# Weight halves for a layer chain: a tile for every weight sum, low parts of down pieces by adding transfers, six whole tiles first

## The reference

```python
def sq_relu_mlp(h, w_up, w_down):
    return jnp.square(jax.nn.relu(h @ w_up)) @ w_down          # hidden width 4096
...
x = x + sq_relu_mlp(rmsnorm(x, mlp_norm[layer]), w_up[layer], w_down[layer])
```

```python
def conv_gated_mlp(n, w_up, conv_w, w_down):
    gate, up = jnp.split(n @ w_up, 2, axis=-1)                 # hidden width 2816
    gate = causal_dwconv(gate, conv_w)                         # 3 taps
    return (jax.nn.silu(gate) * up) @ w_down
```

## Time and profile before

| | |
|---|---|
| median of 3 runs | 2898.85 us (2897.19 to 2899.41) |
| profiled execution, its time | 2896.0 us |
| its span | 2894.2 us |
| PE busy | 2737.9 us (95%) |
| POOL busy | 1879.7 us (65%) |
| DVE busy | 2023.6 us (70%) |
| ACT busy | 1219.6 us (42%) |
| chain that ended last | PE 68%, DVE 22%, issue 5% |
| read from HBM | 249.52 MB |

### The profile page before, as it was taken

The page is one execution under the profiler, slowest core; times in us unless marked ns, Lnnn a source line. Parts: engine busy times, 40 slices in busy tenths (PEclk is TensorE's granted clock), DMA queues, the critical chain, the costliest instruction groups (busy, mean ns, idle before and its releaser), DMA issues.

```text
span 2894.2 us, 48195 instructions
## 1 busy us (share of the span) xinstructions
PE 2737.9 (95%) x18508; PEld 2470.3 (85%) x18508; DVE 2023.6 (70%) x3175; ACT 1219.6 (42%) x2145; POOL 1879.7 (65%) x2144
## 2 busy tenths in 40 slices
PE   9988999999899999999999889999999899988998
PEld 6767989877798988988899888999988799978887
DVE  8958666686666668897544777776797645767775
ACT  4454434455343444433343334445343353334442
POOL 6425998856599885532236589997542225489997
PEclk9999999999999999999999999999999999999999
DMA  5112332332233233323324122233322324122222
GB/s 185 59 34 75 96 110 94 111 102 75 72 100 105 95 117 111 110 66 96 105 83 133 54 81 93 91 100 108 100 78 88 89 87 142 60 86 84 88 90 93
DMA packets 122676, 271.25 MB, mean 94 GB/s; under 512 B 22864, under 2 KB 57040, under 8 KB 122192
## 3 DMA queue, kind: packets, MB, share of 16 engines
q1 hardware_dynamic: 73104, 245.98, 26.4%
q10 hardware_dynamic: 49344, 22.19, 2.8%
HBM read 249.52 MB, written 18.61 MB: 93 GB/s over the span
## 4 chain that ended last, share of the span: by engine, by line
PE 68%; DVE 22%; issue 5%; ACT 2%; POOL 1%; DMA 1%; ACTq 0%; SPq 0%; DVEq 0%
PE aux L1035 16%; PE acc L800 15%; PE acc L1090 13%; PE acc L1287 5%; PE acc L1094 3%; PE acc L849 3%; PE aux L1301 3%; DVE index_score L3227 2%; PE acc L1268 2%; PE aux L1268 2%; DVE best L3220 2%; DVE w_raw L2703 1%; DVE unit_b L3130 1%; POOL w_lo L772 1%; PE acc L833 1%
## 5 line engine op out<-in xcount | busy, mean ns | idle before, releaser
L772 POOL TENSOR_TENSOR w_lo<-w_raw,w_hi 128x256 fp32r<-128x256 f32 x1744 | 1478.5, 881 | 931.9 <-ACT w_hi L1535 928.1
L1535 ACT ACTIVATE w_hi<-w_raw 128x512 fp32r<-128x512 f32 (+2 forms) x680 | 487.2, 738 | 381.6 <-PE acc L800 143.7
L772 POOL TENSOR_TENSOR w_lo<-weight_sum,w_hi 128x256 fp32r<-128x256 f32 x396 | 407.2, 1054 | 61.2 <-ACT w_hi L1535 56.7
L1035 PE MATMUL aux<-token_sum_hi,w_hi 128*128 128x264 f32 (+1 forms) x1056 | 304.7, 289 | 77.6 <-ACT kept_product L1821 40.8
L800 PE MATMUL acc<-n_hi,w_hi 128*128 128x264 f32 (+1 forms) x1336 | 337.6, 317 | 8.8 <-DVE unit_a L3136 6.5
L800 PE MATMUL acc<-n_lo,w_hi 128*128 128x264 f32 (+1 forms) x1336 | 326.6, 309 | 0.0
L800 PE MATMUL acc<-n_hi,w_lo 128*128 128x264 f32 (+1 forms) x1336 | 326.0, 308 | 0.0
L1035 PE MATMUL aux<-token_sum_hi,w_lo 128*128 128x264 f32 (+1 forms) x1056 | 300.5, 285 | 0.0
L1035 PE MATMUL aux<-token_sum_lo,w_hi 128*128 128x264 f32 (+1 forms) x1056 | 300.3, 284 | 0.0
L1035 PEld LDWEIGHTS aux<-token_sum_hi,w_hi 128*128 128x128 f32 x1056 | 201.0, 190 | 90.8 <-issue 67.0
L1090 PE MATMUL acc<-hidden_hi,w_hi 128*128 128x512 f32 x688 | 271.9, 395 | 2.1 <-DVE hidden_lo L3109 2.1
(11 more groups left out here) (525 smaller groups left out, 6364.3 us busy)
## 6 DMA issues: line engine op xcount, KB each, us to landing
w_raw<-in_stream SPq DMA_DIRECT2D x420, 512.0 KB, 3.6
unit_blocks<-unit_scratch ACTq DMA_DIRECT2D x26, 256.0 KB, 3.9
w_raw<-in_stream SPq DMA_DIRECT2D x16, 384.0 KB, 3.2
unit_scratch<-unit_staged ACTq DMA_DIRECT2D x20, 256.0 KB, 2.6
saved_x<-x SPq DMA_DIRECT2D x2, 2112.0 KB, 9.6
x<-saved_x SPq DMA_DIRECT2D x16, 264.0 KB, 2.7
saved_gates<-root ACTq DMA_DIRECT2D x12, 264.0 KB, 2.0
unit_scratch<-unit_staged ACTq DMA_DIRECT2D x1, 2560.0 KB, 15.1
```

Source lines behind the costliest of these rows:

```text
L772: i = pool.tensor_tensor(wl[:, slot, at + a:at + z], source[:, a:z], wh[:, slot, at + a:at + z].bitcast(F32), ALU.subtract)
L1035: mm = pe.matmul(aux[:, bank, 0:width], w[:, slot, at_ + P * b:at_ + P * b + P], v[:, b, :], start=(opens and b == 0 and i == 0), stop=(b ...
L1535: act.activation(wh[:, slot, at_:at_ + n], weights_of(o), ACT.Copy).then_inc(w_hi, 1)
```

## The change

It has four parts.

1. s3 gets a tile of its own (in `square_sum`, which these stages don't use), and a21 is no longer overwritten. In the FFN s3 of the next pair is made behind the second down half, in front of a22's work on DVE; in the MLP it stays at a22. A raw slot of a pair is loaded anew when the four sums are made and the low parts of its direct factors are.
2. The low part of a down half is not subtracted on POOL. ACT writes −w_hi (a rounded copy with scale −1) into `w_lo`, then w_hi; POOL issues a transfer that adds the raw weights from DRAM to it (`accum_op`), with four semaphores in turn, and TensorE waits for its landing. The raw slot is free once ACT has copied both parts.
3. `w_lo` counts only the entries that POOL still subtracts (`order.low`).
4. The MLPs begin with six whole tiles instead of four, and so have 13 pairs instead of 14; the first pair is followed by all eight down halves of the first chunk. DVE's order at the start is written anew. The banks of the down products are counted from the end of the stage.

Some semaphores are merged, two names into one, to make room; each waiter waits for the same event as before.

```diff
+MLP_WHOLE = 6
+def whole_tiles(stage):
+    return MLP_WHOLE if stage.startswith("mlp") else FFN_CHUNKS[0][1]
...
-    order = [("whole", 0, n) for n in range((2 if gated else 1) * chunks[0][1])]
+    order = [("whole", 0, n) for n in range((2 if gated else 1) * whole_tiles(stage))]
     for e in range(1, len(chunks)):
-        n = (chunks[e][1] - chunks[e][0]) // (1 if gated else 2)
+        a = max(chunks[e][0], whole_tiles(stage))
+        n = (chunks[e][1] - a) // (1 if gated else 2)
         for i in range(n):
-            order.append(("pair", e, i))
+            order.append(("pair", a, i))
             order += [("down", e - 1, k) for k in range(4 * i // n, 4 * (i + 1) // n)]
...
+    def parts_of(self, p):
+        return [n for n, (kind, piece, _) in enumerate(self.ops)
+                if (piece == p and kind in ("whole", "down", "a11", "a12")) or (piece == p - 1 and kind == "a22")]
...
+    sum_tiles = {"s1": weight_sum[:, 0, :], "s2": weight_sum[:, 1, :], "s4": weight_sum[:, 2, :], "s3": ssq[:, 0:KT // 2 * P]}
...
         for p in range(RAW_SLOTS, pieces):
-            sp.wait_ge(w_lo, order.freed(p - RAW_SLOTS))
+            q = p - RAW_SLOTS
+            last = order.parts_of(q)[-1]
+            if order.ops[last][0] == "down":
+                sp.wait_ge(w_hi, last + 1)
+            else:
+                sp.wait_ge(w_lo, order.low[last])
+            if q in order.sums or q - 1 in order.sums:
+                sp.wait_ge(w_sum, order.sums[q if q in order.sums else q - 1])
             load_piece(p)
...
+            if kind == "down":
+                d = order.sent[o] - 1
+                if d >= LOWS:
+                    pool.wait_ge(*low_landed(d - LOWS))
+                pool.wait_ge(w_hi, o + 1)
+                pool.dma_start(wl[:, slot, at:at + n], stream[p, :, part * n:part * n + n], accum_op=ALU.add)\
+                    .then_inc(low_landed(d)[0], 16)
+                continue
...
-                pe.wait_ge(w_lo, o + 1)
+                if kind == "down":
+                    pe.wait_ge(*low_landed(order.sent[o] - 1))
+                else:
+                    pe.wait_ge(w_lo, order.low[o])
...
+            if kind == "down":
+                act.activation(wl[:, slot, at_:at_ + n], weights_of(o), ACT.Copy, scale=-1.0)
             act.activation(wh[:, slot, at_:at_ + n], weights_of(o), ACT.Copy).then_inc(w_hi, 1)
...
-                i = dve.tensor_tensor(a21, a21, a11, ALU.subtract)
+                i = dve.tensor_tensor(s3, a21, a11, ALU.subtract)
...
             token_sum_low(stage, 0)
+            whole(2)
+            token_sum_low(stage, 1)
             weight_sum_of(stage, 0, "s1")
-            token_sum_low(stage, 1)
             weight_sum_of(stage, 0, "s2")
-            whole(2)
+            whole(3)
             token_sum_low(stage, 2)
             weight_sum_of(stage, 0, "s4")
             token_sum_low(stage, 3)
+            whole(4)
             weight_sum_of(stage, 0, "s3")
-            whole(3)
+            whole(5)
             low()
...
-                    weight_sum_of(stage, u + 1, "s3")
                     if u == feed["pairs"] - 1:
                         low()
                 elif kind == "down":
                     down(o, d, stage, last_rows(l))
                     d, since = d + 1, since + 1
-                    if since == 1:
-                        weight_sum_of(stage, pair + 1, "s4")
+                    if since in (1, 2):
+                        weight_sum_of(stage, pair + 1, ("s4", "s3")[since - 1])
```

More of the change, by code:

```diff
@@ L136 @@
 LATER = 2
+LOWS = 4
 STAGES = ["mix0", "mlp0", "mix1", "mlp1", "layer0", "layer1"]
@@ L172, in mlp @@
                 for i in range(2):
-                    column("w_up", layer, P * (MLP_CHUNKS[e][0] + 2 * n + i))
+                    column("w_up", layer, P * (e + 2 * n + i))
             else:
@@ L207, in block2 @@
                 for c in (0, FF2):
-                    column("w_up_2", layer, c + P * (FFN_CHUNKS[e][0] + n))
+                    column("w_up_2", layer, c + P * (e + n))
             else:
@@ L282, in __init__ @@
         self.index = {op: n for n, op in enumerate(self.ops)}
+        self.low, self.sent, low, sent = [], [], 0, 0
+        for kind, _, _ in self.ops:
+            low, sent = low + (kind != "down"), sent + (kind == "down")
+            self.low.append(low)
+            self.sent.append(sent)
+        self.sums, sums = {}, 0
+        for feed in self.feeds.values():
+            for q in feed["pieces"]:
+                sums += len(SUMS)
+                self.sums[q] = sums
     def used(self, n):
@@ L297, in half @@
         return self.place[o] // 2, KT // 2 * P * (self.place[o] % 2)
-    def freed(self, p):
-        found = [n + 1 for n, (kind, piece, _) in enumerate(self.ops) if piece == p or (piece == p - 1 and kind == "a22")]
-        paired = [n + 1 for n, (kind, piece, _) in enumerate(self.ops) if piece == p and kind == "s3"]
-        return paired[0] if paired else max(found)
+    def parts_of(self, p):
+        return [n for n, (kind, piece, _) in enumerate(self.ops)
+                if (piece == p and kind in ("whole", "down", "a11", "a12")) or (piece == p - 1 and kind == "a22")]
 PAD = 4
@@ L394, in build @@
     order = Order(plan, starts)
-    used, evicted, slot_of = order.used, order.evicted, order.slot
+    used, evicted, slot_of, lows = order.used, order.evicted, order.slot, order.low
     base = -(-nc.sbuf_base // 64) * 64
@@ L618, in build, with low_landed @@
     x_saved, gate_kept = sem("x_saved"), sem("first_gate_ready")
-    meta_gained, both_sums, x_root = sem("meta_gained"), sem("both_sums_ready"), sem("x_root_ready")
+    meta_gained, both_sums, x_root = sem("meta_gained"), sem("ln_scaled_then_both_sums_ready"), sem("x_root_ready")
     gate_sent = sem("gate_sent")
     gate_back = [sem(f"gate_back_{n}") for n in range(4)]
+    low_of = [sem(f"down_low_landed_{n}") for n in range(LOWS)]
+    def low_landed(d):
+        return low_of[d % LOWS], 16 * (d // LOWS + 1)
     def first(u):
@@ L1079, in pairs_and_downs @@
                     wide_ = stage.startswith("mlp")
-                    pe.wait_ge(taken, done + d - (3 if wide_ else 1))
-                    banks = acc[:, (bank_of(feed["first"] + feed["whole"]) + d) % 4, :] if wide_ else \
+                    pe.wait_ge(taken, done + max(d - (3 if wide_ else 1), 0))
+                    banks = acc[:, (bank_of(feed["end"]) + d - feed["downs"]) % 4, :] if wide_ else \
                         acc[:, 2 * ((pair_of(feed["first"] + feed["whole"]) + d) % 2):][:, 0:2]
@@ L1660, in copy_v @@
             def copy_v(pair):
-                act.wait_ge(vt_full, pair + 1)
+                act.wait_ge(vtok_full, c.next(vtok_full))
                 act.activation(vt[:, :, P * pair:P * pair + P], acc[:, 1, :].rearrange("p (a d) -> p a d", a=4),
@@ L1711, in mixer0 @@
                         act.wait_ge(cent_ready, c.next(cent_ready))
-                        act.activation(zpad[:, i, 0:SEQ], cv[:, i, :], ACT.Square).then_inc(ln_sq, c.made(ln_sq))
+                        act.activation(zpad[:, i, 0:SEQ], cv[:, i, :], ACT.Square).then_inc(vtok_ready, c.made(vtok_ready))
                 if n == 13:
@@ L2286, in _ @@
         c = Counts()
-        at = {"piece": 0, "squared": False, "low": 0, "split": [0, 0, 0, 0]}
+        at = {"piece": 0, "squared": False, "low": 0}
         def step(i):
@@ L2481, in mixer0 @@
                 if n == 12:
-                    dve.wait_ge(mean_full, 1)
+                    dve.wait_ge(gcol_full, c.next(gcol_full))
                     for i in range(4):
@@ L2572, in square_of_mult @@
             def square_of_mult(h):
-                dve.wait_ge(tanh_ready, h + 1)
+                dve.wait_ge(first_tap, c.next(first_tap))
                 dve.wait_ge(a_ready, 2 * h + 1)
@@ L2689, in weight_sum_of @@
                     dve.wait_ge(landed[q % RAW_SLOTS], 16 * (q // RAW_SLOTS + 1))
-            if name != "s3" and at["split"][n]:
-                dve.wait_ge(w_lo, at["split"][n])
-            at["split"][n] = order.index[name, p, u] + 1
+            if u:
+                dve.wait_ge(w_lo, order.low[order.index[name, feed["pieces"][u - 1], u - 1]])
             if name in ("s2", "s4"):
                 dve.wait_ge(*at["sum"])
-            s1, s2, s4 = (weight_sum[:, k, :] for k in range(3))
+            s1, s2, s4, s3 = (sum_tiles[k] for k in SUMS)
             if name == "s1":
@@ L2720, in down @@
             if stage.startswith("mlp"):
-                a = acc[:, (bank_of(p) + d) % 4, :]
+                a = acc[:, (bank_of(order.feeds[stage]["end"]) + d - order.feeds[stage]["downs"]) % 4, :]
             else:
```

61 lines of the change are left out of this document (29 added, 32 removed).

## The result

The changed kernel takes 2873.21 us (median of 4 runs, 2869.70 to 2877.81) against 2898.02 us for the kernel before on the same chip: a ratio of 0.9913, 95% interval 0.9900 to 0.9925. It is 24.8 us faster, where the prediction said 54. The profiled execution took 2870.28 us, its span is 2868.5.

The account below looks back on a forecast made before the run. Bounds: in the FFN the chain through the late s3 (period 17.3 us, TensorE's work 16.1), in the MLPs only where pairs begin. 2896.0 − 40.7 − 14.6 = 2840.7, plus 2.85 to the median, say 2844; range 2822 to 2892.

Parts of the forecast that it names:

- The FFN's sum: FFNs of both layers: s3 made sooner cuts the period from 17.3 to 16.3 us over 19 pairs each; gain 40.7 us.
- Landing ... Cost 0 to 0.1: FFN down halves: adding transfers land in 3.6 to 3.9 us, about when TensorE needs them; cost 0 to 0.1.
- 3 and 4 us where pairs begin: FFNs: TensorE idle time still left where pairs begin, beside 0.25 and 0.45 us a pair in layers 0 and 1.
- The slack of 3.8 us: FFN: of 8.8 us from a22's end to the first down half, 3.8 remain for landing after s3's low part and issue.
- the rival that put 46 us on a landing of 5 us: FFN: landing at 5 us stalls 1.2 us a pair, 38 pairs, giving 2890; late landing's chance 0.10, half of it no change.
- a full POOL alone does not explain idle time: Kernel before: POOL is 93 to 95% busy in MLP and FFN stretches alike, yet the first MLP's body has no idle.
- at an unchanged 21.0 us: MLP bodies: a sign of being right, POOL under 90% busy while the period stays at TensorE's own 21.0 us.
- from 0.28 to 0.33 busy by at most a third more bytes: DMA engines: adding transfers raise their busy share of 0.28 to 0.33 by at most a third; raw loads not late.
- The rival that GpSimd's issue is dear: POOL's issues: at 1.5 us the FFN's 40.7 are gone, at 1.89 the kernel is 16 slower, 2915; chance 0.15.
- priced at 74 us: FFN: GpSimd issues starved by DVE, two held a full instruction each, add 1.9 us a pair, 74 in all.
- Six whole tiles: MLP starts: lost time falls from 12.15 and 11.65 to 4.1 and 2.5, less 1.3 us each; gain 14.6 us.
- too short to bring the clock down: MLP starts: TensorE's remaining wait of 2.5 us (1.5 to 4) does not lower its clock as 8.64 did.

Follow-up runs that it names:

- experiment 1: Changed kernel with adding transfers in the two layers alone; MLP down pieces' low parts made by GpSimd again: 2860.61 us, ratio 0.9871.
- experiment 4: Changed kernel with four whole tiles and no adding transfers, all low parts on POOL, s3 still sooner in its own tile: 2887.50 us, ratio 0.9967.
- experiment 7: Changed kernel with the layers' s3 made behind the gated tile again, still in its own tile, transfers kept: 2941.09 us, ratio 1.0152.
- (6): Changed kernel with the MLPs' adding transfers made plain copies of the same bytes, so results there are not the reference's: 2865.91 us, ratio 0.9894.
- (8): experiment 1 with adding transfers also for the first half of each MLP down piece, GpSimd for the second: 2868.34 us, ratio 0.9906.
- (2): Changed kernel whose MLP load queue asks for the first down piece before the next pair's second piece: 2869.41 us, ratio 0.9899.
- Experiments 9: experiment 1 with ScalarE taking high parts of the sixth tile, a11 and first sums sooner at each MLP's start: 2867.44 us, ratio 0.9898.
- experiment 11: Experiment 9's kernel with ScalarE also copying the products of a11 and s1 ahead of the last hidden tile: 2863.10 us, ratio 0.9882.

## Why the prediction was wrong

**The FFN's sum (forecast 40.7, measured 33.9): right in mechanism, short in size.** The period came to 16.3 and 16.2 us, for which 16.3 was forecast. But the forecast gave this gain to all 19 pairs. The first six periods of layer 0's FFN, where the chunks are short, took 112.7 us before and 112.6 after. Two terms were too small there. One is "Landing ... Cost 0 to 0.1". The transfers take 5.4 us from issue to landing in layer 0's FFN, not the 3.6 to 3.9 of the earlier trace rows, and TensorE waited for them: in experiment 1, where only the layers have such transfers, 7.7 us in one form of down product and 6.1 in the other, 13.8 in all. The other is "3 and 4 us where pairs begin": before the third pair's a22 TensorE now waits 5.4 us in layer 0 and 3.4 in layer 1 for DVE, 2.5 and 2.6 before. The slack of 3.8 us was nearly enough; the rival that put 46 us on a landing of 5 us overdrew it, since it charged every pair.

**Which part gave it.** The prediction booked the gain to the sooner sum and gave the transfers no part but to keep POOL out of the way. The runs show that neither does it alone. The sum alone gives 10.5 of the 33.9 (experiment 4), for POOL's 18 subtractions fill 17.2 us. The transfers without the sum lose 43 us in all and 36 in the FFNs (experiment 7), for ACT then has five copies where it had three between the late sum and the kept product. The prediction had both facts in hand: POOL at 93 to 95% in the earlier trace rows, and the five copies at 2.8 us; it read the first as "a full POOL alone does not explain idle time", which is true and beside the point: it was the next bound, 0.1 to 0.3 us under the old period.

**The adding transfers at no cost in the MLPs: the step that failed.** The prediction keeps the period "at an unchanged 21.0 us". It says that the DMA engines go "from 0.28 to 0.33 busy by at most a third more bytes; raw loads are not late for it". The bytes were 29.05 MB for 21.03 in 200 us, 38% more and near enough. The time of the engines was not: 0.33 became 0.62, since an adding transfer costs 3.13% per MB where a load costs 1.56. The loads landed 8.2 us after their issue, and the MLPs took 13.1 us more than with these transfers in the layers alone (experiment 1); 10.2 of it went with the adding itself (experiment 6). The starts of a22 on TensorE show where it was lost, mlp0 / mlp1, in us:

| | stage's first instruction to first a22 | to second a22 | the later periods, over 21.0 each |
|---|---|---|---|
| no such transfers in the MLPs (experiment 1) | 49.7 / 47.5 | 32.2 / 32.1 | 0.0 / 0.0 |
| plain copies (6) | 50.4 / 49.5 | 32.1 / 32.1 | 0.0 / 0.0 |
| half of them (8) | 54.0 / 49.8 | 32.2 / 32.1 | 0.0 / 0.0 |
| all, other order of loads (2) | 50.8 / 49.5 | 34.5 / 33.5 | 0.7 / 0.3 |
| all (changed kernel) | 51.3 / 49.9 | 33.9 / 33.0 | 4.0 / 1.8 |
| all (experiment 7, same MLPs) | 51.2 / 49.4 | 34.0 / 33.1 | 2.0 / 9.2 |

So the periods are stretched only with all the transfers and with loads that land in 8.2 us; where they landed in 5.6 (experiments 2 and 8) they were in time, or nearly. With all of them the stretch with the eight down halves in a row, behind the first pair, costs another 0.9 to 2.3 us in each MLP; TensorE waits there for landings and for DVE. Of the 4.1 us that the changed kernel is later at the first a22, 1.6 are the clock in mlp0; of the rest, in mlp1, 1.7 are waits for ACT's copies of kept products, 1.6 with plain copies and none in experiment 1. The late landing was foreseen for the added transfers and put among the rivals; what it does to other transfers was not. Two of the prediction's own signs of being wrong came true: TensorE waiting on DMA in down, and MLP periods above 21.0. The rival that GpSimd's issue is dear is out: 1.11 us median for the 224 issues, as taken, with a longest of 3.6:

```profile
L805 POOL DMA_DIRECT2D w_lo<-in_stream x224 | 215.3, 1144 | 59.5 <-DMA w_lo<-in_stream 38.4
```

The 38.4 us at its end are the limit of four outstanding transfers, which holds POOL back when they land late; what that costs TensorE was not separated. The warning in the Trainium skill (SBUF — State Buffer, SBUF: two separate sides) of issues starved by DVE, priced at 74 us in the prediction, did not come true at that size.

**Six whole tiles (forecast 14.6, measured 5.2).** The prediction followed the first sum s1 and found it 2.5 us late; it was not what came last. Two more tiles put the sixth tile's split behind ACT's copies for the token sums, and its low part into the time in which DVE never pauses. The wait of 3.0 us there was followed by the lower clock in both MLPs of the changed kernel, which "too short to bring the clock down" denied; in mlp0 of experiment 1 the same wait was not. Experiments 9 and 11 show that without this wait others take its place, so the sixth tile is only the first of several things that are late there.

Sum of the misses: 6.8 in the FFNs, 9.4 for the six whole tiles, 13.1 for the transfers in the MLPs, 29.3 of the 29.6 us between 2843.6 and 2873.2.

**The fastest kernel** is that of experiment 1, 2860.61 us: the sooner sum, six whole tiles, and adding transfers where they relieve an engine that is full and nowhere else. It is 12.6 us faster than the changed kernel and 37 faster than the one before; experiment 11, at 2863.10, is not clearly slower.

## What to carry to other kernels

Count a transfer that adds as twice its bytes of DMA time, and ask first what it does to the loads that share the engines, not when it lands itself. A load has slack, so this cost nothing in the periods up to a landing of 5.6 us and then several us at 8.2. Moving work off an engine is worth something only where that engine binds: the same edit gave 21 to 23 us in the FFNs and took some 12 in the MLPs. Before booking a gain to one edit, find the next bound under the old period and see which edit lifts it; two edits that each free one engine can be worth little or less than nothing alone.

## What the runs showed of the hardware

- Adding transfers from GpSimd's queue took 3.13% of the 16 DMA engines per MB, plain copies of the same bytes from the same queue 1.76, SP's loads 1.5 to 1.6. Landing of 256 KB, median: 8.2 us adding and 5.6 plain in the body of mlp0.
- With all of them in, 512 KB loads of another queue landed in 8.2 us instead of 3.7, at a DMA share of 0.62 in the mean over mlp0's body; in single slices of 5 us it was 0.9 or more.
- A POOL subtraction of 128x256 took 1.64 us in a row of six (9.85 us) at 261.66 in the changed kernel, and 0.79 in a row of four (3.15 us) at 249.43 in experiment 1. DVE was busy without a gap beside both, in the first mostly on operations that read two tiles, in the second, for about half of the time, on one that reads a single tile. The Trainium skill (SBUF — State Buffer, Who interferes with whom) says that a DVE operation on two tensors, both in SBUF, contends with GpSimd's reads. The two rows agree with it in direction; no run here varies DVE's work alone.
- TensorE's clock was at its lower level for some 3.6 us behind a wait of 3.01 us that followed on unbroken work, in mlp0 of the changed kernel. In mlp0 of experiment 1 it stayed at 1.00 behind a wait of 3.02 us in the same place.
